# Moving one slab's low part on VectorE: from before the heads of a latent attention to the sixth step of its loop

## The reference

```python
q = (cq @ w_uq).reshape(bsz, seq, MLA_HEADS, QK_NOPE + QK_ROPE)
k_nope = jnp.einsum("bsc,chd->bshd", ckv, w_uk)
v = jnp.einsum("bsc,chd->bshd", ckv, w_uv)
...
s = (jnp.einsum("bqhd,bkhd->bhqk", qn, k_nope)
     + jnp.einsum("bqhd,bkd->bhqk", qp, k_pe)).astype(jnp.float32) * scale
p = jax.nn.softmax(jnp.where(allowed[None, None], s, -jnp.inf), axis=-1).astype(v.dtype)
o = jnp.einsum("bhqk,bkhd->bqhd", p, v)
...
return o @ w_o
```

## Time and profile before

| | |
|---|---|
| median of 3 runs | 1078.43 us (1078.33 to 1079.07) |
| profiled execution, own time | 1078.6 us |
| its span in the records | 1076.8 us |
| TensorE matmuls busy | 1067.1 us, 99% |
| TensorE weight loads busy | 926.9 us, 86% |
| VectorE busy | 702.8 us, 65% |
| ScalarE busy | 550.3 us, 51% |
| GpSimd busy | 47.4 us, 4% |
| DMA | 201.68 MB, 187 GB/s mean |
| TensorE clock granted | 90% of full speed or more in each of 40 slices |

### The profile page before, as it was taken

The page is one execution under the profiler, slowest core; times in us unless marked ns, Lnnn a source line. Parts: engine busy times, 40 slices in busy tenths (PEclk is TensorE's granted clock), DMA queues, the critical chain, the costliest instruction groups (busy, mean ns, idle before and its releaser), DMA issues.

```text
span 1076.8 us, 14947 instructions
## 1 busy us (share of the span) xinstructions
PE 1067.1 (99%) x5901; PEld 926.9 (86%) x5901; DVE 702.8 (65%) x788; ACT 550.3 (51%) x651; POOL 47.4 (4%) x87
## 2 busy tenths in 40 slices
PE   8999999999999999999999999999999999999998
PEld 7888888888998888888878888889998888888886
DVE  4778756566776765656586555555888767555563
ACT  5563644444468454444465444445756746444443
POOL 1001000000200100000010000001040100000000
PEclk9999999999999999999999999999999999999999
DMA  9864765554572486665557655654784357655521
GB/s 312 295 217 151 254 184 185 191 188 154 142 265 72 164 264 191 195 195 194 160 192 236 191 175 186 194 153 134 215 253 165 118 168 236 200 180 186 193 107 39
DMA packets 138975, 201.68 MB, mean 187 GB/s; under 512 B 9144, under 2 KB 112800, under 8 KB 138928
## 3 DMA queue, kind: packets, MB, share of 16 engines
q1 hardware_dynamic: 136000, 191.25, 55.5%
q0 software_dynamic: 2928, 9.79, 2.7%
HBM read 199.95 MB, written 1.06 MB: 187 GB/s over the span
## 4 chain that ended last, share of the span: by engine, by line
PE 96%; DVE 2%; ACT 1%; issue 0%; POOL 0%; ACTq 0%; DVEq 0%; POOLq 0%
PE up L1865 26%; PE up L1868 14%; PE acc L1876 12%; PE acc L1877 12%; PE acc L1879 12%; PE up L1816 2%; PE up L1817 2%; PE up L1818 2%; PE acc L2004 2%; PE acc L1996 2%; PE acc L1995 2%; PE up L1938 1%; PE acc L2346 1%; PE up L2186 1%; PE up L1842 1%; PE up L1852 1%
## 5 line engine op out<-in xcount | busy, mean ns | idle before, releaser
L1205 DVE TENSOR_TENSOR weight_lo<-raw,weight_hi 128x2048 fp32r<-128x2048 f32 (+4 forms) x184 | 411.3, 2239 | 110.0 <-ACT weight_hi L642 109.8
L642 ACT ACTIVATE weight_hi<-raw 128x2048 fp32r<-128x2048 f32 (+4 forms) x184 | 343.4, 1869 | 154.3 <-PE acc L1879 146.2
L1865 PE MATMUL up<-x_parts,weight_hi 128*128 128x512 f32 x1232 | 307.5, 391 | 0.0
L1865 PEld LDWEIGHTS up<-x_parts,weight_hi 128*128 128x128 f32 x1232 | 224.5, 188 | 42.2
L1868 PEld LDWEIGHTS up<-x_parts,weight_lo 128*128 128x128 f32 x1232 | 168.1, 190 | 12.0
L1876 PE MATMUL acc<-weight_hi,hh 128*128 128x512 f32 x448 | 175.3, 391 | 0.0
L1877 PE MATMUL acc<-weight_lo,hh 128*128 128x512 f32 x448 | 175.0, 391 | 0.0
L1868 PE MATMUL up<-x_parts,weight_lo 128*128 128x256 f32 x1232 | 171.8, 282 | 0.0
L1879 PE MATMUL acc<-weight_hi,hl 128*128 128x512 f32 x448 | 138.5, 390 | 0.0
L642 ACT ACTIVATE tmp_a<-up 128x512 f32<-128x512 f32 x52 | 31.0, 597 | 148.0 <-PE up L1868 148.0
L1879 PEld LDWEIGHTS acc<-weight_hi,hl 128*128 128x128 f32 x448 | 84.1, 188 | 17.9
(11 more groups left out here) (278 smaller groups left out, 1094.4 us busy)
## 6 DMA issues: line engine op xcount, KB each, us to landing
raw<-in_ff_w SPq DMA_DIRECT2D x64, 1024.0 KB, 5.5
raw<-in_ffn_w_down SPq DMA_DIRECT2D x22, 1024.0 KB, 4.9
raw<-in_ffn_w_gate SPq DMA_DIRECT2D x20, 1024.0 KB, 5.4
raw<-in_ffn_w_up SPq DMA_DIRECT2D x20, 1024.0 KB, 5.3
raw<-in_w_in SPq DMA_DIRECT2D x14, 1024.0 KB, 5.6
raw<-in_sc_w_in SPq DMA_DIRECT2D x11, 1024.0 KB, 8.6
raw<-in_w_out SPq DMA_DIRECT2D x6, 1024.0 KB, 5.9
raw<-in_sc_w_out SPq DMA_DIRECT2D x4, 1024.0 KB, 6.2
```

Source lines behind the costliest of these rows:

```text
L642: return nc.scalar.activation(dst, src, ACT.Copy, **kw)
L1205: return vec.tensor_tensor(dst, whole, high.bitcast(F32), ALU.subtract)
L1865: mm(bank.rearrange("p (a n) -> p a n", a=2), w_h[k], x_parts[:, k, :, :], start=k == 0, stop=k == KD - 1, skip_group_check=True)
```

## The change

The call that splits slab `WO + 1` (written `UQ + 3 + RING`) is taken from in front of the heads and made in iteration 5 of DVE's loop instead, the sixth, behind `output_a(2)` and ahead of `scaled_a(5)`, which opens iteration 6. Nothing else is changed; the number and the shapes of the instructions are the same. As a line is gone, the lines behind 1519 have numbers lower by one.

```diff
                 if j == 3:
                     split_slab(UQ + 2 + RING)
                 rotate(j + 1, [(q_rot[:, j, :], slice(0, P))])
-            split_slab(UQ + 3 + RING)
...
-                if h in (7, 8):
-                    split_slab((UK, UV)[h - 7] + RING)
+                if h in (5, 7, 8):
+                    split_slab((UQ + 3, 0, UK, UV)[h - 5] + RING)
                 if h == 9:
                     split_slab(WO + RING)
```

## The result

| | before | the change |
|---|---|---|
| median of 22 runs each, us | 1078.37 | 1080.05 |
| lowest to highest, us | 1078.05 to 1080.71 | 1079.60 to 1081.52 |
| ratio, 95% interval | | 1.0016, 1.0010 to 1.0021 |
| profiled execution: own time, span, us | 1078.6, 1076.8 | 1080.05, 1078.3 |

The account below looks back on a forecast made before the run. TensorE, busy 99% of the span, was taken to bound the kernel, in a ring without slack with VectorE. Terms of -0.09 us at the front and +1.71 in the sixth step gave +1.62, so 1080.1 us, range 1079.2 to 1081.0.

Parts of the forecast that it names:

- The front: Ahead of the heads: removing the split brings the turn of head 2 only 0.09 us earlier, as VectorE then waits for scores.
- The sixth step: VectorE's loop: the moved split delays the reciprocal and turn of head 5 by 1.71 us; only 0.41 us of it hides.
- The sum: Whole kernel: -0.09 + 1.71 = +1.62 us, giving 1080.1 us, 0.15% slower.
- The ring: Loop of the heads: TensorE's turn follows VectorE's scaling by 0.07 us, so there is no slack and nothing is won back.
- hidden: Rival in the loop: VectorE's idle time takes up the split, about 1078.2 us; chance 0.06 together with a half way.
- The rule on the drain: Sixth step: the next operation waits for the emptied pipe, making the term 1.87 instead of 1.71 us; not adopted.
- Queues at nothing: Queues the step is moved past: cost 0, the later load of `WO + 5` having 15 us of cover.
- The chain's reading: Rival: the split at the front wins 2.20 us and only 1.71 is lost, 1077.9 us; chance 0.03.
- The second stall: Rival at the turn of head 6: scaling or ScalarE's copy is late once more, 1080.6 to 1081.1 us; chance 0.08.
- The clock: Rival: TensorE idles some 1.6 us and then gets 1.2 instead of 2.4 GHz, 1082.4 to 1087.9 us; chance 0.03.

Follow-up runs that it names:

- quarters: The change with the moved split in four pieces of 512 columns, at the ends of the iterations for heads 2 to 5: 1078.42 us, ratio 1.0002.
- load_held: Kernel before, VectorE's order kept; only SyncE holds the load of `WO + 5` until the output's low part in the sixth step: 1078.31 us, ratio 1.0003.
- little_sixth: The change with the moved split cut to 64 of its 2048 columns: 1078.21 us, ratio 1.0001 against the kernel before.
- little_front: Kernel before with the split at the front cut to 64 of its 2048 columns: 1078.25 us, ratio 0.9997.
- end7: Against the kernel before, the whole front split moved to the end of the iteration for head 7: 1079.21 us, ratio 1.0009.
- half_more: The change with another half split (1024 columns) ahead of the moved one: 1082.94 us, ratio 1.0039 against the kernel before.
- twice_sixth: The change with the moved split made twice, the second behind the first: 1084.75 us, ratio 1.0058 against the kernel before.
- second group: Follow-up kernels trying where a split costs and how much, run on one chip beside the kernel before, whose median there was 1078.40 us.
- third_step: Against the kernel before, the whole front split moved to the end of the iteration for head 2: 1079.86 us, ratio 1.0016.
- first group: Follow-up kernels trying the split's two places and the load, run on one chip beside the kernel before, whose median there was 1078.41 us.

## Why the prediction was right, point by point

The first point rests on one more row of the kernel before, the maxima of head 2 on VectorE:

```profile
330.45 0.61 DVE L1524 TENSOR_REDUCE head_max<-up 128x1 f32<-128x128 f32 x2
```

- **The front: -0.09 us predicted, about -0.01 found.** This is the term that was mis-sized. I took the maxima of head 2 to start at 330.53 in the kernel before, "when the copy ended". They really started at 330.45 (the row above), 0.05 us behind the end of the scores at 330.40 and 0.08 before the record of the copy ends. In the change they start at 330.23, 0.04 behind scores that end at 329.96 + 0.23 = 330.19. The maxima of head 0 did come 0.36 us earlier, as worked out (321.76, and 0.21 for the shifted stretch, is 321.97), and all of it turned into VectorE's wait for TensorE. A start should have been read from its own row, and not from the end of the row before it. For the ring I did so; at the front I did not.
- **The sixth step: +1.71 predicted, 1.69 found.** From turn 2 to turn 5 it is 341.13 - 332.63 = 8.50 us, before 339.66 - 332.85 = 6.81. The succession of 2.54 us was right to the hundredth, and TensorE followed the scaling after 341.13 - 341.08 = 0.05 us instead of 0.07. One sentence beside the term was wrong: not 0.41 us of the split hide, but 2.20 - 1.71 = 0.49, as the split too overlaps its neighbour's record by 0.08.
- **The sum.** -0.01 + 1.69 = 1.68 us for 1.62. The two errors, 0.08 and 0.02, go opposite ways, so by a little luck the sum is off by 0.06 us and not by 0.1.
- **The ring.** "VectorE's idle time looks like room": for a whole split it was none beyond the idle time ahead of the reciprocal, and the ring won nothing back (the shift is 1.68 us at turn 5, 1.69 at turn 6, 1.68 at `WO + 5`). The *hidden* rival falls for the change. In pieces the room exists, as quarters shows, so its reading was right of the step and wrong of the instruction.
- **The rule on the drain.** The recorded split ends 0.09 us after the next instruction starts (338.14 + 2.28 = 340.42, next start 340.33), as before to 0.01 us. The rule of the Trainium skill (VectorE: DVE Perf Modes, section The DRAIN you can't avoid) that the next operation waits for the emptied pipe would have made 1.87 us of 1.71; 1.69 was measured. The same section adds that an operation which is not held starts earlier. So the rows do not speak against the page, but the price of 1.87 was wrong for this split. Whether the chip holds an operation here, no run shows.
- **Queues at nothing.** Shown by load_held and little_sixth, and by ScalarE's unchanged 7.89 us.
- **The chain's reading** falls by little_front: 2.2 us on the chain, 0.01 in the time.
- **The second stall** did not come: turn 6 has no wait. ScalarE's copy of the turned head 5 does stand behind the exponentials of head 6, at 342.44, and nobody waits for it.
- **The clock** stayed full in the profiled execution. My grounds for a small chance were thin: half a split more was enough to lose the clock, and the wait that I named as passed at full clock, 1.77 us, was not passed so in every execution (end7, under **Open**). The Trainium skill (TensorE: Matmul & The Clock Gate, section HAM oscillation) has the mechanism right, idle time of TensorE and then half the clock; half_more and twice_sixth show it at 1.6 and 2.4 us on top of the stall, where the rival had 2.3 to 7.8 (1082.4 to 1087.9 less 1080.1).

**Open.** Five of the change's 22 runs lie at 1080.83 to 1081.52 us, 0.8 to 1.5 above the median, with mean granted clocks of 0.997 to 0.999; of before's 22 two do, 1.1 and 2.3 us above theirs. In the second group third_step has three such runs in 11 and end7 two, while before has none in 33. But in the first group before has four in 27 at 1.4 to 2.1 above its median, and load_held, which adds no wait for TensorE, four in 11 at 1.2 to 1.6.

One such run has a trace: the profiled execution of end7, 1080.35 us with a mean granted clock of 0.997. TensorE at its start, and two stages:

```profile
9.79 1.60 PE L1843 MATMUL up<-x_parts,weight_hi 128*128 128x256 f32 x8 [1.85 <-ACT weight_hi L642]
```

```profile
10.00:12.00 2.00, 2.00 (x12) 2.00 (x12) 1.49 (x2) 1.06 (x1) 1.39 (x3) 0.58 1.09 351
12.00:14.00 2.00, 2.00 (x13) 2.00 (x12) 0.64 (x1) 0.37 (x1) 0.90 (x2) 0.56 1.11 351
```

The three groups of matmuls from 9.79 on take 14.23 - 9.79 = 4.44 us; the same three take 13.02 - 10.08 = 2.94 in the kernel before. Every stage from 14 us to past the heads shows 1.00. So this execution lost its extra time behind the wait at 9.79 us, 300 us ahead of the heads, and not at the moved split. The other eleven traces have the same wait, 1.77 to 2.00 us long, and 1.00 in the stages behind it. So a wait of this kind was passed at full clock in eleven executions of twelve, and its length alone does not decide. Whether the change's five runs lost their time at the start too, or now and then at the new wait of 1.54 us, is not shown: none of them has a trace.

## What to carry to other kernels

In a loop whose step is a ring through several engines, price an added instruction by the idle time just ahead of the one it delays, both taken from start to start, and not by the engine's busy share; then cut it into pieces that fit the idle time of a step, or put it ahead of an instruction that waits for another engine anyway. Before booking a gain for work taken off the chain of waits, look for what the next engine waits for second: here scores that ended only 0.05 us before they were used made 2.2 us worth nothing. And take the price of a short wait of TensorE as its length only where traces show waits as long passed at full clock, and in more than one execution: the 1.85 us of end7 were not, the 2.00 us at the same place in load_held were.

## What was not expected of the hardware

- The clock's price is small but starts early. The stall with a wait of 2.79 us cost 1.6 us more than itself, the one of 3.86 us 2.4 more; in both the clock came back to 2.4 GHz within the stages shown, while TensorE was working without a gap. In half_more it fell only after TensorE had resumed, so the row of the wait itself still shows 1.00; in end7 it fell behind the wait as well.
- At 1.2 GHz two score products behind turn 5 start 0.42 us apart (344.00, 344.42) where it is 0.23 in the change (341.51, 341.74), and VectorE got a wait of 1.00 us for TensorE in twice_sixth: at the slow clock the ring waited for TensorE.
- The end of a record is not the earliest start of the next one on the same engine. The split's neighbour starts 0.09 us before the split's record ends (340.33 against 340.42), and the maxima of head 2 start 0.08 us before that of the copy (330.45 against 330.53). There the scores had ended 0.05 us earlier, so which of the two let the maxima go cannot be told from these rows.
